# Dense product with the whole table of v for blocks 1 to 3, gathered rows of v for the others

## The reference

```
a   = einsum('phkd,pd->phk', u_table[ex], hx)       # 128 rows of u for each token
act = gelu(a) * softmax gate
out = einsum('phk,phkd->pd', act, v_table[ex])       # 128 rows of v for each token
x   = x + gt2 * out;  y = rmsnorm(x, g_final)
```

## Time and profile before

| | |
|---|---|
| median of 3 runs | 3583.11 us |
| profiled execution | 3583.99 us |
| its span, first to last instruction | 3582.2 us |
| bytes moved by DMA | 1251.85 MB, 349 GB/s in the mean |
| read from HBM, written | 1228.70 MB, 21.67 MB |
| instructions | 30420 |

### The profile page before, as it was taken

The page is one execution under the profiler, slowest core; times in us unless marked ns, Lnnn a source line. Parts: engine busy times, 40 slices in busy tenths (PEclk is TensorE's granted clock), DMA queues, the critical chain, the costliest instruction groups (busy, mean ns, idle before and its releaser), DMA issues.

```text
span 3582.2 us, 30420 instructions
## 1 busy us (share of the span) xinstructions
PE 2246.2 (63%) x9719; PEld 980.1 (27%) x9719; DVE 2134.7 (60%) x4860; ACT 361.4 (10%) x755; POOL 2292.5 (64%) x2229
## 2 busy tenths in 40 slices
PE   7582895668748888666467777444445444454566
PEld 6472552135413344211124444011011111011111
DVE  2355877665576666575764556766666666665301
ACT  2111241001120122100000010000000000000000
POOL 0123556766677766676766676777777777777665
PEclk9796998789969999788678888776676666767799
DMA  7767868999999999899999999999999999999998
GB/s 233 184 234 246 296 215 311 393 369 400 380 382 404 406 347 355 316 397 377 384 368 378 370 386 367 364 367 376 370 383 369 379 368 374 364 365 356 364 372 308
DMA packets 372669, 1251.85 MB, mean 349 GB/s; under 512 B 37879, under 2 KB 41359, under 8 KB 372495
## 3 DMA queue, kind: packets, MB, share of 16 engines
q0 software_dynamic: 304784, 1109.40, 82.2%
q1 hardware_dynamic: 45551, 96.47, 7.7%
q10 hardware_dynamic: 22176, 44.04, 3.3%
HBM read 1228.70 MB, written 21.67 MB: 349 GB/s over the span
## 4 chain that ended last, share of the span: by engine, by line
POOL 30%; PE 26%; DMA 19%; issue 14%; DVE 6%; another core or an unknown queue 3%; ACT 1%; DVEq 1%; SPq 0%; POOLq 0%; ACTq 0%
POOL v_ring L804 16%; POOL u_ring L787 14%; DMA v_ring<-in_v_table_dram,eidt 13%; PE bank L1701 11%; PE bank L1537 4%; PE bank L1619 4%; DVE u_ring L1340 3%; DMA u_ring<-in_u_table_dram,eid 3%; PE bank L1520 3%; PE bank L1595 2%; DMA u_ring<-in_v_table_dram,eidt 1%; DMA wring<-in_w_ada_dram 1%; POOL u_ring L804 1%; PE bank L1635 0%
## 5 line engine op out<-in xcount | busy, mean ns | idle before, releaser
L1701 PE MATMUL bank<-v_ring,act_x 128*32 128x512 f32 x3984 | 1205.1, 822 | 980.3 <-DMA v_ring<-in_v_table_dram,eidt 879.3
L1340 DVE CUSTOM_DVE_ANT_0 u_ring<-u_ring,h 128x1024 f32<-128x1024 f32 x1056 | 1279.9, 1225 | 899.1 <-DMA u_ring<-in_u_table_dram,eid 719.1
L787 POOL DMA_INDIRECT u_ring<-in_u_table_dram,eid x1024 | 1106.8, 1081 | 530.5 <-issue 301.3
L804 POOL DMA_INDIRECT v_ring<-in_v_table_dram,eidt x996 | 1075.4, 1080 | 565.3 <-issue 253.2
L1701 PEld LDWEIGHTS bank<-v_ring,act_x 128*32 128x32 f32 x3984 | 269.3, 136 | 1829.7 <-issue 1820.9
L1619 PE MATMUL bank<-hbuf,wring 128*128 128x128 f32 (+1 forms) x2048 | 258.8, 281 | 48.4 <-issue 46.6
L1619 PEld LDWEIGHTS bank<-hbuf,wring 128*128 128x128 f32 x2048 | 244.7, 196 | 84.1 <-issue 83.7
L1537 PE MATMUL bank<-zc,dring 128*128 128x384 f32 x496 | 198.1, 527 | 16.9 <-ACT dring L834 13.4
L1520 PE MATMUL bank<-hbuf,wring 128*128 128x384 f32 (+2 forms) x512 | 165.6, 482 | 15.5 <-ACT hbuf L847 10.5
L1363 DVE TENSOR_TENSOR scratch<-bank,mod 128x512 f32<-128x512 f32 x18 | 11.6, 687 | 189.9 <-PE bank L1701 188.6
L1595 PE MATMUL bank<-wring,mixt 128*128 128x512 f32 (+1 forms) x256 | 123.0, 631 | 1.1 <-DMA wring<-in_w_out_dram 1.1
(11 more groups left out here) (225 smaller groups left out, 1621.5 us busy)
## 6 DMA issues: line engine op xcount, KB each, us to landing
u_ring<-in_u_table_dram,eid POOLq DMA_INDIRECT x1024
wring<-in_w_out_dram ACTq DMA_DIRECT2D x16, 1024.0 KB
wring<-in_w_query_dram ACTq DMA_DIRECT2D x16, 1024.0 KB
v_ring<-in_v_table_dram,eidt POOLq DMA_INDIRECT x996
v_ring<-in_w_ada_dram SPq DMA_DIRECT2D x11, 1024.0 KB, 10.7
wring<-in_w_ada_dram SPq DMA_DIRECT2D x10, 1024.0 KB
wring<-in_w_in_dram ACTq DMA_DIRECT2D x10, 1024.0 KB
xr<-in_x_prompt_dram SPq DMA_DIRECT2D x16, 512.0 KB
```

What stands on the lines that cost most here:

```text
L787: pool.indirect_dma_start(u_ring[:, n % NU], None, u_table[0], bass.IndirectOffsetOnAxis(ap=col, axis=0)).then_inc(u_in[n % NU], 16)
L804: pool.indirect_dma_start(place, None, v_table[0], bass.IndirectOffsetOnAxis(ap=eidt[:, b % RING, t:t + 1], axis=0)).then_inc(landed, 16)
L1340: dve.tensor_tensor_reduce(u_ring[:, n % NU], u_ring[:, n % NU], h2[:, b % 2], 1.0, 0.0, ALU.mult, ALU.add, dot[:, b % 2, k:k + 1]).then_i ...
L1701: last = pe.matmul(acc[h][j * S:(j + 1) * S, :], act_x[:, i % 2, j, a:a + S], v_place(n)[0][:, h * HALF:(h + 1) * HALF], start=(c == 0), s ...
```

## The change

Blocks 1, 2 and 3 no longer gather rows of v. Instead their weights are written into three matrices in DRAM, `w_dram[d]`, of 16384 experts x 128 tokens, and the result is the product of this matrix with the whole table of v.

- In slots 18 to 29 of stage 0, SP writes zeros over the three matrices (`w_clear`, 24 DMAs of 1 MB).
- In stage b + 1, after DVE's `weigh` of block b, POOL adds the weights into the matrix (`put`): 128 indirect DMAs with `compute_op=ADD`, each moving one float of each partition to the address expert x 128 + token. `PUT_AT` spreads them over slots 2 to 31, four or five behind each slot's four gathers of u. Before every 16th but the first, POOL waits for all earlier ones to land.
- From slot 161 on (stage 5), SP loads the matrices (three DMAs of 512 KB for each of 16 groups, `w_load`) and the table of v (64 DMAs of 1 MB, 8 KB per partition, `v_load`) into the buffers that the mixer no longer needs, and PE multiplies (`dense`): 192 steps of four matmuls 128x128 by 128x512, two steps a slot, in slots 161 to 256.
- Block 0 gathers its rows of v in stage 1, as before. Blocks 4 to 8 gather theirs after the last row of u (`V_TAIL`), with twelve buffers. Their weights and numbers wait in buffers of their own (`actts`, `eidts`), three pairs of banks hold sums (`ACC`), and the `finish` of blocks 1 to 8 stands at the end.
- The room of slots from 65 on is 6 in place of 4.5 and 4.1, so the mixer of the third group is done earlier (its last step moves from slot 164 to 139).

```diff
-ROOM = [None, 4.5, 4.1]
+DENSE = [1, 2, 3]
+GATHER = [b for b in range(NB + 1) if b not in DENSE]
+VI = {b: i for i, b in enumerate(GATHER)}
+ND = len(DENSE)
+DI = {b: i for i, b in enumerate(DENSE)}
+NE = P * P
+WG = 8
+NWG = NE // (P * WG)
+VS = 2
+NVT = NE // (P * VS)
+D_AT = (DENSE[-1] + 2) * NCH
 MAXP = 3 * P
 MAXN = MAXP + S
...
-            while load[at] >= (room if at >= NCH else 8):
+            while load[at] >= (room or (8 if at < NCH else 4.5 if at < V0_END else 6)):
...
+    fill([("dense", i, j, d) for i in range(NWG) for j in range(WG // VS) for d in range(ND)], D_AT + 1, 7)
...
+V0_END = 2 * NCH + 1
+V_AT = {}
+for c_ in range(NCH):
+    V_AT.setdefault(NCH + c_, []).append((0, c_))
+V_TAIL = [(b, c) for b in GATHER[1:] for c in range(rows(b) // CH)]
+PUT_AT = [[k for k in range(P) if k * (NCH - 2) // P + 2 == c] for c in range(NCH)]
...
+        eidts = [eidt[:, :]] * 2 + [s_out[:, :, :, :].rearrange("p a b m -> p (a b) m")[:, i].bitcast(U32) for i in range(4)]
+        actts = [actt[:, :]] + [qt[:, :, :, :].rearrange("p a b t -> p (a b) t")[:, i] for i in range(5)]
...
+        wt = [m[:, 0:ND * WG * P].rearrange("p (d s t) -> p d s t", d=ND, s=WG) for m in (hbuf[:, :], mixt[:, :, :].rearrange("p a n -> p (a n)"))]
+        vt = [wring[:, i].rearrange("p k n -> p (k n)").rearrange("p (s d) -> p s d", s=VS) for i in range(2)]
+        vt += [xr[:, :, :], keyt[:, :, :].rearrange("p a k -> p (a k)").rearrange("p (s d) -> p s d", s=VS)]
+        NVP = len(vt)
...
+        ACC = {b: ps[2 * i:2 * i + 2] for i, b in ((0, 0), (0, 1), (1, 2), (2, 3), (0, 4), (1, 5), (2, 6), (0, 7), (1, SB))}
+        ACC_FREE = {4: 2, 5: 3, 6: 4, 7: 5, SB: 6}
...
+                elif kind == "dense" and step[3] == ND - 1:
+                    n = step[1] * (WG // VS) + step[2]
+                    if n + NVP < NVT:
+                        transfers[s_ + 1].append(("vt", n + NVP))
+                    if n % (WG // VS) == WG // VS - 1 and step[1] + 2 < NWG:
+                        transfers[s_ + 1].append(("wt", step[1] + 2))
+        transfers[D_AT + 1].insert(0, ("dense",))
+        for i in range(ND * 8):
+            transfers[NCH // 2 + 2 + i // 2].append(("zero", i))
+        transfers[V0_END + 4].append(("y", 0))
...
-        V_LAST, U_ALL = LAST * P + CH * (NSG + 2), NB * P + NSG * CH
+        V_LAST, U_ALL = P + CH, NB * P + NSG * CH
...
+            def w_clear(i):
+                sp.wait_ge(x_zero, 1)
+                sp.dma_start(w_dram[i // 8].rearrange("(r p x) o -> r p (x o)", r=8, p=P)[i % 8], xflat[:, 0:NE // 8]).then_inc(w_zero, 16)
+            def w_load(i):
+                if i >= 2:
+                    sp.wait_ge(d_used, (i - 1) * (WG // VS))
+                for d in range(ND):
+                    sp.dma_start(wt[i % 2][:, d].rearrange("p s t -> p (s t)"), w_dram[d].rearrange("(i p x) o -> i p (x o)", p=P, x=WG * P)[i]
+                                 ).then_inc(wt_in[i % 2], 16)
+            def v_load(n):
+                if n >= NVP:
+                    sp.wait_ge(d_used, n - NVP + 1)
+                i, j = n // (WG // VS), n % (WG // VS)
+                sp.dma_start(vt[n % NVP], v_table[0].rearrange("(i p j s) d -> i j p s d", p=P, j=WG // VS, s=VS)[i, j]).then_inc(vt_in[n % NVP], 16)
+            def dense_start():
+                sp.wait_ge(q_ps, len(SCORES))
+                sp.wait_ge(s_ps, len(SCORES))
+                sp.wait_ge(st_ps, 4)
+                sp.wait_ge(st_stored, 16 * (4 + 2 * NS))
+                sp.wait_ge(h2_ps, NB + 1)
+                sp.wait_ge(h2_stored[0], 16 * 4)
+                sp.wait_ge(h2_stored[1], 16 * 3)
+                sp.wait_ge(w_put, 16 * ND * P)
+                w_load(0)
+                for n in range(NVP):
+                    v_load(n)
+                w_load(1)
 
 
...
-                n = b * P + i
+                n = VI[b] * P + i
                 if i == 0:
-                    pool.wait_ge(eidt_ready, b + 1)
+                    pool.wait_ge(eidt_ready, VI[b] + 1)
...
+            def put(b, k):
+                d = DI[b]
+                if k == 0:
+                    pool.wait_ge(wd_ready, d + 1)
+                    pool.wait_ge(w_zero, 16 * 8 * ND)
+                elif k % K == 0:
+                    pool.wait_ge(w_put, 16 * (d * P + k))
+                pool.indirect_dma_start(w_dram[d], bass.IndirectOffsetOnAxis(ap=waddr[:, d, k:k + 1], axis=0), actd[:, d, k:k + 1], None,
+                                        compute_op=ALU.add).then_inc(w_put, 16)
 
...
-                    for j in range(CH):
-                        if p:
-                            v_fetch(p - 1, c * CH + j)
+                    for b, vc in V_AT.get(p * NCH + c, []):
+                        for j in range(CH):
+                            v_fetch(b, vc * CH + j)
+                    if p - 1 in DI:
+                        for k in PUT_AT[c]:
+                            put(p - 1, k)
...
-            for i in range(S):
-                v_fetch(NB, i)
+            for b, vc in V_TAIL:
+                for j in range(CH):
+                    v_fetch(b, vc * CH + j)
...
+                if b in DI:
+                    dve.wait_ge(gel_ready, PARTS * (b + 1))
+                    dve.tensor_tensor(actd[:, DI[b]], dot[:, b % 2], gate[:, b % RING].rearrange("p h k -> p (h k)"), ALU.mult)
+                    dve.tensor_scalar(work[:, 0:P], eidf[:, b % 3], float(P), tcol[:, :], ALU.mult, ALU.add)
+                    dve.drain()
+                    dve.tensor_copy(waddr[:, DI[b]], work[:, 0:P])
+                    dve.drain().then_inc(wd_ready, 1)
+                    return
...
-                dve.wait_ge(v_free, P * (b + 1) if b < NB else P * NB + S)
+                if b in DI:
+                    dve.wait_ge(d_done, DI[b] + 1)
+                else:
+                    dve.wait_ge(v_free, P * VI[b] + rows(b))
...
-                            last = pe.matmul(acc[h][j * S:(j + 1) * S, :], act_x[:, i % 2, j, a:a + S],
+                            n = VI[b] * P + 4 * c + j
...
+            def dense(i, j, d):
+                n = i * (WG // VS) + j
+                if j == 0:
+                    pe.wait_ge(wt_in[i % 2], 16 * ND * (i // 2 + 1))
+                if d == 0:
+                    pe.wait_ge(vt_in[n % NVP], 16 * (n // NVP + 1))
+                if n == 0 and d == 0:
+                    pe.wait_ge(acc_free, 1)
+                    pe.wait_ge(qt_ready, len(SCORES))
+                    pe.wait_ge(st_ready, 4)
+                for s in range(VS):
+                    for h in range(2):
+                        last = pe.matmul(ACC[DENSE[d]][h][:, :], wt[i % 2][:, d, j * VS + s, :], vt[n % NVP][:, s, h * HALF:(h + 1) * HALF],
+                                         start=(n + s == 0), stop=(n == NVT - 1 and s == VS - 1))
+                if n == NVT - 1:
+                    last.then_inc(d_done, 1)
+                elif d == ND - 1:
+                    last.then_inc(d_used, 1)
...
-            for c in range(NSG):
-                tokens(NB, c)
+            for v in V_TAIL:
+                tokens(*v)
```

More of the change, by code:

```diff
@@ L702, in _ @@
                     h2_load(p + 1)
-                if s % NCH == 3 and p >= 2:
-                    y_store(p - 2)
-                    y_load(p - 1)
-            y_store(LAST)
+            for b in range(1, NB):
+                y_store(b)
+                if b < LAST:
+                    y_load(b + 1)
             sp.wait_ge(x1_stored[SB % 2], 16 * (SB // 2 + 1))
@@ L1090, in _ @@
             take_weights(NB)
-            spread(NB, 0)
-            fin_root(LAST)
+            for b, vc in V_TAIL:
+                if vc in SPREAD_AT and (b < NB or vc == 0):
+                    spread(b, SPREAD_AT.index(vc))
+                if vc == 2:
+                    for a in DENSE if b == GATHER[1] else [b - 1]:
+                        fin_root(a)
             fin_root(NB)
```

125 lines of the change are left out of this document (82 added, 43 removed).

## The result

The changed kernel takes 4096.28 us (median of 4 runs, 4085.24 to 4107.52), the one before 3586.54 us beside it: a ratio of 1.1425, 95% interval 1.1386 to 1.1464, 14% slower. The forecast was 3847 us, 7% slower, with a range of 3680 to 4200. The sign and the order of the stages came out. In the profiled executions the forecast had a loss of 264 us and 501 came: one term was too small by 242 us. The profiled execution took 4085.24 us, its span is 4082.7.

A forecast was written before the change was run, and what follows sets the result against it. The prediction took gathered bytes on DMA to bound the kernel. Its terms, 982 + 20 + 1150 + 855 + 50 + 767 + 21 = 3845 us, with 1.79 around the span gave 3847 us, 7.3% slower, range 3680 to 4200.

The forecast's parts named there:

- What bounds: Kernel before: bound by gathered bytes on DMA while both tables are fetched; a pair of gathers costs about 3 us.
- Zeros, 20 us: Stage 0: writing 24 MB of zeros exceeds idle DMA time and adds 20 us, bounds 0 and 65.
- Stages 2 to 4, 1150 us: POOL ends last with 128 gathers of u and 128 puts at 1.365 us each, plus waits: 383 us a stage.
- The waits, 21 x 4.9 us: Stages 2 to 4: every 16th put waits for earlier ones to land, seven times a block, 4.9 us each.
- Stages 5 to 7, 855 us: PE 232, DMA 266 and DVE 267 us overlap with 18 us loss: 285 us a stage, before 1117 in all.
- The tail, 767 us: After the last gather of u: 544 gathers of v alone, DMA-limited at 1.41 us each, bounds 751 and 794 us.
- (c): Rival, stages 2 to 4: POOL at undisturbed 1.24 us, waits covered by gathers of u; total 3651 us; chance 0.11.
- (a): Rival, stages 2 to 4: puts dearer than a gather, on DMA or POOL; total between 4050 and 4400 us; chance 0.20.
- (b): Rival, stages 2 to 4: puts cheap at 0.55 us, DVE's 280 us a stage decide; total 3537 us, 1.3% faster; chance 0.06.
- (d): Rival, stages 5 to 7: PE doesn't hold its clock; at the lower level 537 us more, total 4384 us; chance 0.05.

## Why the prediction was right in sign and too small

**What bounds.** Right. The kernel before is a queue of gathers on DMA; the run with only the tail moved shows that moving them out from beside the work costs 5.9% by itself.

**Zeros, 20 us.** Too much: stage 2 starts at 982.6 us, and stage 1 shows no loss either. They fit into idle time of DMA, the lower bound.

**Stages 2 to 4, 1150 us: the term that was mis-sized.** The mechanism was right (POOL ends last, DVE's work is covered), the price of a put was wrong. It was taken from the gather, 1.065 us, because both make 128 descriptors from 128 numbers; a put lasts 1.867. The packets on q0 agree with the reason, 144 for either, but the time doesn't follow them: the addition comes on top. The 242.4 us split up as: puts 384 x (1.867 - 1.065) = +308; gathers of u 384 x (0.999 - 1.065) = -25; waits for own DMA 46.6 instead of 103, -56; waits for DVE +18; gaps -3. The nearest row was near only to what the instruction costs without the addition (1.24 us in the mean, 0.97 at the shortest). For a gather and a put together the forecast had 2.99 us (383 over 128) with an upper bound of 4.25; measured are 3.63 us (1392.4 over 384), halfway between. The forecast had named this case itself: a stage of over 450 us means that the put has to be looked at, and a stage took 464.

**The waits, 21 x 4.9 us.** 18 were seen with 46.6 us, 2.6 each. In these 18 the waiting put stands right behind another put, and from the start of that one to its own start 3.1 to 7.4 us pass, 4.5 in the mean. So the landing was priced about right. But 1.9 us of it pass in the put's own instruction, which the sum had counted already; that was left out. In the other three (number 64 of each block) four gathers stand between, over 6.9 us had passed, and nothing was left to wait for. The estimate by the Trainium skill (page "DMA: Bandwidth & Descriptors", section "Anatomy of one DMA — SWDGE (gpsimd) path") was 42 us in all and lies closer than mine, but by luck. Its 2.0 us stand for the whole of such a DMA, and no wait here shows them: the shortest is 3.1 us.

**Stages 5 to 7, 855 us.** 847.5. The sum held, its parts only half: without the dense product a stage takes 257 us and not DVE's 267, and the meeting of three queues costs 26 and not 18. The two errors cancel in part, which is luck. PE's price came from matmuls with a tile of 32 columns, not of 128; it did no harm, PE was busy 221 us a stage against 232. PE was busy 78% at a granted clock of 0.89, a little below the "over 80%" and "above 0.9" that I asked for. Of the 77 us that the dense product costs, 72.5 are DVE's waits for rows of u.

**The tail, 767 us.** 791.7, 1.455 us a gather in place of 1.41. The 1.41 was 90 us over 64 issues. Issues run ahead of bytes, and the same row had 364 GB/s: 0.524 MB at that rate is 1.44 us, 783 us for 544. The changed kernel's tail moved 373 GB/s at a DMA share of 0.99, and at its two ends DMA wasn't full. The other rule that I had weighed, the Trainium skill's 358 GB/s from HBM for a core (page "DMA: Bandwidth & Descriptors", section "Where 436 GB/s comes from"), gave 797 us, an estimate. It fits the sum better than it fits the rate: 373 GB/s were moved here and 407 on chip B, so it isn't a ceiling in either run.

**Slips that carry no weight.** A gather's 1.42 us of DMA came from 2080 gathers; there are 2112, which makes it 1.39 us, and 535 us for 384 in place of 544. The prediction says that the range down to 3680 us keeps most of (c), whose own total was 3651, outside it. And the errors of the terms other than stages 2 to 4 (-19.4, -7.5, -2.5 and +24.7 us) cancel by luck.

**The rivals.** (a), puts dearer than a gather with a total between 4050 and 4400, is what happened, in its variant on POOL: the instruction was longer by 0.80 of the 1.365 us that I doubled. It had 0.20. What should have raised it: the trace showed plain DMAs and gathers alone, and nothing with an addition, so the middle of the bounds had as good a claim as the lower part. (b), cheap puts with 3537 us, was right about the rest of the kernel, though only once the mixer is spread out: without puts, 3542.63 us on chip C, 1.4% faster than before (0.7 to 2.2%). So the gain that the dense product could bring with puts at no cost is 1.4% on this chip, none on chip B (1.2% slower), and the changed kernel takes 16% more than that (4112.2 over 3542.63), of which the packing is at most 57 us. (c) falls with the price; (d) did not occur: in stages 5 to 7 PE was granted 0.89.

**Where the gain of 384 fewer gathers went.** Their 535 us of DMA time are gone. In stages 2 to 4 the saving was never to be had in full, since without any puts they still take 837 us at a DMA share of 0.84; with puts they take 1392 at 0.62. A gather of v costs DMA 1.39 us; the put that replaces it costs POOL 2.16 us with its gap, beside 1.3 us for each gather of u. As long as every put stands beside a gather of u, the pair is 3.5 us of POOL, before any wait, where two gathers were about 3 us of DMA. In stages 5 to 7 POOL waits 260.5 us for DVE; whether puts spread into them, with the dense product later, would gain anything was not tried.

Not tried: several puts in one instruction, a shorter wait between puts (their order on the same matrix rests on it), and rows of v of block 4 beside the dense product, whose accumulators take the banks that it would need.

## What to carry to other kernels

Before work is moved off a full queue, price the replacement on the engine that issues it: instruction plus gap, times the count, in the stage where it runs. An operation that the trace has not shown (here a DMA that adds) belongs between its bounds, not at the price of its nearest plain relative; one small run of it would have told. And when transfers are taken out of a stage, look at what else fills that stage's transfer time: what DMA doesn't fetch beside the work, it fetches behind it. A rate is read from bytes over time; a count of issues in a window reads too fast.

## What was not expected of the hardware

- An indirect DMA of one float a partition keeps POOL for 1.87 us in the mean when it adds, 1.24 when it stores, 1.19 when it reads, and 1.55, 0.97 and 0.94 at the shortest. A gather of 4 KB a partition takes 0.94 at its shortest as well, so for POOL the bytes cost nothing and the addition 0.6 us.
- With the addition a put makes 144 packets on its queue, without it 32; a gather of rows makes 144 too.
- Three chips gave 3563.64, 3412.49 and 3589.2 us for the same kernel, a spread of 5%, and a tail gather of 1.32 to 1.33 us on the second against 1.44 to 1.46. POOL-bound stages differed by less than 0.5% (1390.3, 1392.4, 1396.0 us).
- What lengthens POOL's indirect DMAs goes with DVE's work. In stages 2 to 4 the mean gather of u is 999 ns where DVE is busy 0.55 of the time (adding puts), 1051 at 0.61 (storing puts), 1065 at 0.64 (before), 1168 at 0.70 (half of the puts) and 1371 at 0.82 (no puts, chip C). In the tail of the changed kernel, where DVE is nearly idle and DMA at 0.99, a gather is 0.95 us in the mean, so it isn't the load of DMA. The starts and ends in the traces show the same for single instructions:

| stages 2 to 4, mean of one, us (count) | DVE busy under 5% of it | DVE busy over 95% of it |
|---|---|---|
| gather, kernel before | 0.94 (176) | 1.17 (263) |
| gather, no puts, chip C | 0.94 (7) | 1.57 (193) |
| storing put | 0.98 (26) | 1.32 (119) |
| adding put | 1.56 (38) | 1.98 (101) |

No run changed DVE's work alone, so that it is the cause is not shown.
